# Block 2's stage meetings and mixers: low parts of the second unit last, another order of attention steps, lighter VectorE work, rotary row swaps by DMA

## The reference, cut to what matters

```python
def second_block(x, c, ...):
    for l in range(2):
        h = _rmsnorm(x, norm_g[l, 0]) * (1.0 + sc0) + sh0
        x = x + 0.5 * g0 * _swiglu(h, ...)
        h = _rmsnorm(x, norm_g[l, 1]) * (1.0 + sc1) + sh1
        x = x + g1 * _token_mix(h, ...)
        h = _rmsnorm(x, norm_g[l, 2]) * (1.0 + sc2) + sh2
        x = x + 0.5 * g2 * _swiglu(h, ...)

def _rope(x, pos):                       # d = 32 or 64, half = d // 2
    x1, x2 = xf[..., :half], xf[..., half:]
    return jnp.concatenate([x1 * cos - x2 * sin, x2 * cos + x1 * sin], axis=-1)

def _diff_attention(q, k, v, lam, ...):  # 4 heads, two maps of 32 rows each
    s = jnp.einsum('bhmqd,bhmkd->bhmqk', qi, k) * scale
    p = _masked_softmax(s, causal)
    a = p[:, :, 0] - lam * p[:, :, 1]
    return a @ v

def _compress(x, pe, w1, w2):
    return jax.nn.silu(flat @ w1) @ w2

def _nsa(q, kc, vc, ks, vs, kw, vw, gates, pe, w1, w2):
    q = _rope(q); k_slc = _rope(ks); k_win = _rope(kw)
    k_cmp, v_cmp = _rope(_compress(kc)), _compress(vc)
    # compressed branch: masked softmax over 31 blocks (a row that sees none gives 0)
    # two more branches: causal softmax with k_slc and with k_win
    return g0 * o_cmp + g1 * o_slc + g2 * o_win
```

## Time and profile before

| | before |
|---|---|
| median of 3 runs | 2774.49 us |
| the profiled execution | 2776.58 us |
| its span | 2775.2 us |
| PE busy | 2712.5 us (98%) |
| DVE busy | 1667.2 us (60%) |
| ACT busy | 1024.0 us (37%) |
| mean granted TensorE clock | 0.992 |

### The profile page before, as it was taken

One profiled execution on the slowest core, in us unless ns is written; L12 is line 12 of the kernel. 1 busy time (PEld: TensorE's weight loads), 2 busy tenths in 40 slices (PEclk: granted clock), 3 DMA queues, 4 the chain that ended last, 5 costly groups with the idle time before them and its releaser, 6 DMA issues.

```text
span 2775.2 us, 35300 instructions
## 1 busy us (share of the span) xinstructions
PE 2712.5 (98%) x14529; PEld 2218.1 (80%) x14529; DVE 1667.2 (60%) x3377; ACT 1024.0 (37%) x1745; POOL 15.8 (1%) x47
## 2 busy tenths in 40 slices
PE   8999999999999999889999999999999989999999
PEld 5788888899888897666888889888888666888888
DVE  6776555357766456778776736753355778633334
ACT  4642332444222244455422224322234455422223
POOL 1000000000000000000000000000000000000000
PEclk9999999999999999999999999999999999999999
DMA  7246333224555232200555524533232310233231
GB/s 249 91 167 184 107 92 98 76 92 167 187 188 186 84 118 80 84 32 31 182 182 183 196 84 139 202 122 106 91 104 89 94 43 31 68 96 102 92 102 65
DMA packets 340360, 325.24 MB, mean 117 GB/s; under 512 B 9442, under 2 KB 332774, under 8 KB 340200
## 3 DMA queue, kind: packets, MB, share of 16 engines
q1 hardware_dynamic: 340116, 322.97, 36.1%
q10 hardware_dynamic: 84, 0.02, 0.0%
HBM read 320.87 MB, written 2.10 MB: 116 GB/s over the span
## 4 chain that ended last, share of the span: by engine, by line
PE 88%; DVE 7%; ACT 3%; SPq 1%; issue 0%; DMA 0%; DVEq 0%
PE bank L535 25%; PE bank L537 24%; PE bank L536 24%; PE bank L577 3%; PE bank L563 2%; PE bank L564 2%; PE bank L565 2%; PE bank L2319 1%; PE bank L2348 1%; DVE w_lo L503 1%; ACT E L2122 1%; PE bank L1373 1%; PE bank L1363 1%; DVE tmp L713 1%; DVE h_lo L702 1%; DVE E L2445 0%
## 5 line engine op out<-in xcount | busy, mean ns | idle before, releaser
L535 PE MATMUL bank<-h_lo,w_hi 128*128 128x512 f32 (+1 forms) x2448 | 929.4, 380 | 7.7 <-DVE h_lo L702 7.3
L537 PE MATMUL bank<-h_hi,w_lo 128*128 128x512 f32 (+1 forms) x2448 | 902.1, 369 | 0.0
L536 PE MATMUL bank<-h_hi,w_hi 128*128 128x512 f32 (+1 forms) x2448 | 901.1, 368 | 0.0
L503 DVE TENSOR_TENSOR w_lo<-raw,w_hi 128x1024 fp32r<-128x1024 f32 (+1 forms) x422 | 490.8, 1199 | 300.9 <-ACT w_hi L497 300.7
L497 ACT ACTIVATE w_hi<-raw 128x1024 fp32r<-128x1024 f32 (+1 forms) x422 | 421.5, 1035 | 341.9 <-PE bank L537 326.6
L535 PEld LDWEIGHTS bank<-h_lo,w_hi 128*128 128x128 f32 x2448 | 463.0, 189 | 94.7 <-issue 10.3
L536 PEld LDWEIGHTS bank<-h_hi,w_hi 128*128 128x128 f32 x2448 | 463.0, 189 | 79.3 <-issue 7.2
L537 PEld LDWEIGHTS bank<-h_hi,w_lo 128*128 128x128 f32 x2448 | 462.1, 189 | 77.5
L535 PE MATMUL bank<-a_lo,w_hi 128*128 128x512 f32 (+1 forms) x1056 | 390.8, 370 | 0.0
L537 PE MATMUL bank<-a_hi,w_lo 128*128 128x512 f32 (+1 forms) x1056 | 384.6, 364 | 0.0
L536 PE MATMUL bank<-a_hi,w_hi 128*128 128x512 f32 (+1 forms) x1056 | 384.4, 364 | 0.0
(11 more groups left out here) (311 smaller groups left out, 2600.1 us busy)
## 6 DMA issues: line engine op xcount, KB each, us to landing
swf<-in_w_ada SPq DMA_DIRECT2D x60, 1024.0 KB, 7.5
raw<-in_ffn_w_gate SPq DMA_DIRECT2D x44, 1024.0 KB, 5.4
raw<-in_ffn_w_up SPq DMA_DIRECT2D x44, 1024.0 KB, 5.4
raw<-in_w_in SPq DMA_DIRECT2D x40, 1024.0 KB, 5.1
raw<-in_ffn_w_down SPq DMA_DIRECT2D x32, 1024.0 KB, 5.0
raw<-in_w_in SPq DMA_DIRECT2D x34, 512.0 KB, 5.0
raw<-in_ffn_w_down SPq DMA_DIRECT2D x16, 768.0 KB, 4.2
mw<-in_w_mod SPq DMA_DIRECT2D x8, 1024.0 KB, 11.3
```

The source lines that it names most:

```text
L503: nc.vector.tensor_tensor(o, r, half(w_his[place_of[i]], i, h)[0].bitcast(F32), ALU.subtract).then_inc(*w_lo.up((i, h)))
L535: nc.tensor.matmul(o, w1, al, start=start, stop=False)
L536: nc.tensor.matmul(o, w1, ah, start=False, stop=False)
L537: return nc.tensor.matmul(o, w2, ah, start=False, stop=stop)
```

## The change

1. **Meetings.** `dve_w` of the second unit leaves slot 6 of `dve_modulate` and stands behind its last chunk.
2. **Rotary part of nq, ks and kw (six of ten units in each mixer).** The matmul is gone. SP copies the rows with four DMAs inside SBUF, 32 rows of 512 columns each, to `swap`, and the sign is in the sin table. DVE multiplies `swap` by sin and adds. For ks and kw one 128x512 sum goes out, and SP copies the second head group to the other half of the partitions with two DMAs each (`sp_cross`).
3. **Differential attention.** DVE makes the factors of step s-1 between map 0 and map 1 of step s; ACT scales map 0 of step s-1 between the two exponentials of step s, ahead of its copy.
4. **Silu of the hidden layer.** ACT makes it as Exp, Ln(1+z), Exp; two DVE instructions fall away. The second one comes a step earlier on ACT.
5. **Compressed branch.** `VB` is one 128x512 product with a quadrant mask in place of eight copies and POOL's clearing; the 0/1 mask over 256 columns becomes a factor of the 8 sums.

```diff
@@ dve_second, dve_to_h
-                3: [lambda: update(6)], 4: [lambda: dve_nacc(st, 6, 1)], 5: [lambda: update(7)],
-                6: [lambda: st != "end" and dve_w(first_of(st)[1], 0)]}
+                3: [lambda: update(6)], 4: [lambda: dve_nacc(st, 6, 1)], 5: [lambda: update(7)],}
...
             dve_modulate(st, 0, mu, add, dve_second(st, b4, gain))
+            dve_w(first_of(st)[1], 0)
@@ rope
+    def sp_rope(l, p):
+        sp.wait_ge(act, ("rq", l, p))
+        for i in range(4):
+            nc.sync.dma_start(swaps[p % 2][i * 32:i * 32 + 32, :], pair(p)[0][(i ^ 1) * 32:(i ^ 1) * 32 + 32, :]).then_inc(
+                *swap_in[p % 2].up((l, p), 16))
...
+        else:
+            q0 = swaps[p % 2]
+            dve.wait_ge(swap_in[p % 2], (l, p))
+            nc.vector.tensor_tensor(q0[:, :], q0[:, :], sin, ALU.mult).then_inc(*dve.up(("rs", l, p)))
@@ dve_da, act_da
+                    if m:
+                        factors(s - 1)
...
-                dve.wait_ge(act, ("de", l, n, 1))
-                nc.vector.reciprocal(st[:, 2:4], st[:, 2:4]).then_inc(*dve.up(("dr", l, n)))
-                dve.wait_ge(dve, PREV)
-                nc.vector.tensor_tensor(st[:, 3:4], st[:, 3:4], lv[:, 6:7], ALU.mult).then_inc(*dve.up(("dl", l, n)))
-                dve.wait_ge(dve, PREV)
+                dve.wait_ge(dve, ("dl", l, n))
...
+                    if m:
+                        first_map(s - 1)
@@ silu
+        act.wait_ge(act, PREV)
+        nc.scalar.activation(z, z, use(ACT.Ln), bias=ones[0:64, 0:1]).then_inc(*act.up(("h4", l, m)))
+        act.wait_ge(act, PREV)
+        nc.scalar.activation(z, z, use(ACT.Exp), scale=-1.0).then_inc(*act.up(("hs", l, m)))
...
-        nc.vector.tensor_scalar(z, z, 1.0, None, ALU.add).then_inc(*dve.up(("h3", l, m)))
-        nc.vector.reciprocal(z, z).then_inc(*dve.up(("h4", l, m)))
@@ dve_vc, dve_nsa
-                nc.vector.tensor_copy(VB[g][r, q * 64:q * 64 + 64], ps.of(("hv", l))[r, g * 64:g * 64 + 64]).then_inc(
+        nc.vector.tensor_tensor(VB[:, :].rearrange("p (g q d) -> p g q d", g=2, q=4),
...
-                nc.vector.tensor_tensor(e3, e3, c01, ALU.mult).then_inc(*dve.up(("cz", l, b)))
@@ pe_mixer
-        pe_rope(l, 4)
         compressing(0, 0)
-        pe_rope(l, 5)
@@ sp_mixer
+        swap_after = {("nq", l, 0): (4, 5), ("nq", l, 1): (6, 7), ("kk", l): (8, 9)}
         for n in names[index["dk", l]:index["vv", l]]:
             sp_raw(index[n] + 2)
+            for p in swap_after.get(n, ()):
+                sp_rope(l, p)
+            if n == ("ng", l):
+                sp_cross(l)
+    def sp_cross(l):
+        for n, kd in enumerate((ks, kw)):
+            sp.wait_ge(dve, ("rd", l, 8 + n))
+            for par in range(2):
+                r, o = slice(par * 64, par * 64 + 64), slice(64 - par * 64, 128 - par * 64)
+                nc.sync.dma_start(kd[r, 512:1024], kd[o, 0:512]).then_inc(*cross_in[n].up(l, 16))
```

More of the change, by code:

```diff
@@ L52, in host_constants @@
     c["ca"] = m(ok).transpose(1, 0, 2).reshape(128, 128)
-    c["c01"] = ok.astype(np.float32).transpose(1, 0, 2).reshape(128, 128)
+    c["any"] = ok.any(2).astype(np.float32).T
+    c["quad"] = (p[:, None] // 32 == np.arange(4)[None, :]).astype(np.float32)
     res = np.concatenate([c[n] for n in RES], 1)
@@ L69, in table @@
         return np.ascontiguousarray(co.T[rows]), np.ascontiguousarray(si.T[rows])
-    l2 = np.concatenate([*table(64, np.arange(S)), *table(64, end)], 1)
+    co, si = table(64, np.arange(S))
+    si = np.where((p % 64 < 32)[:, None], -si, si)
+    l2 = np.concatenate([co, si, *table(64, end)], 1)
     return {"k_res": res.astype(np.float32), "k_l1": l1.astype(np.float32), "k_l2": l2.astype(np.float32),
             "k_da": np.concatenate(table(32, np.arange(S)), 1)}
-RES = ["ident", "ones", "bones", "tril", "C", "R32", "R64", "ca", "c01"]
-RESW = {"C": 512}
+RES = ["ident", "ones", "bones", "tril", "C", "R32", "R64", "ca", "any", "quad"]
+RESW = {"C": 512, "any": 4, "quad": 4}
 PREV = "prev"
@@ L373, in build @@
     kcz = here("kcz", 128)
-    VB = [here(f"VB{i}", 256) for i in range(2)]
+    VB = here("VB", 512)
     hid, hsum = [here(f"hid{i}", 128) for i in range(2)], here("hsum", 256)
@@ L389, in build @@
     dk = sb("dk", 1024, at=at_a + 8192)
+    swaps = [sb(f"swap{i}", 512, at=at_a + 16384 * i + 12288) for i in range(2)]
     groups = vector_rows(A)
@@ L1957, in build @@
     ld_ws, ld_bs = sig("ws_in"), sig("bs_in")
+    swap_in = [sig(f"swap{i}_in") for i in range(2)]
+    cross_in = [sig(f"cross{i}_in") for i in range(2)]
     PAIR = {("dq", 0): 0, ("dq", 1): 1, ("dk", 0): 2, ("dk", 1): 3, ("n0", 0): 4, ("n0", 1): 5, ("n1", 0): 6,
@@ L1978, in rope_where @@
         else:
-            kd = (ks, kw)[p - 8]
-            d = [(slice(g * 64, g * 64 + 64), kd[par * 64:par * 64 + 64, g * 512:g * 512 + 512])
-                 for g in range(2) for par in range(2)]
+            d = [(every, (ks, kw)[p - 8][:, 0:512])]
         return t, d
@@ L1992, in pe_rope @@
         pe.wait_ge(act, ("rq", l, p))
-        nc.tensor.matmul(t[:, :], rope_where(l, p)[0][0], pair(p)[0][:, :], start=True, stop=True).then_inc(
+        nc.tensor.matmul(t[:, :], cst["R32"], pair(p)[0][:, :], start=True, stop=True).then_inc(
             *pe.up(("rr", l, p)))
     def dve_rope(l, p):
-        (_, cos, sin), dsts = rope_where(l, p)
+        (cos, sin), dsts = rope_where(l, p)
         q0, q1 = pair(p)
@@ L2079, in dve_da, with factors @@
     def dve_da(l):
+        def factors(n):
+            if n < 0:
+                return
+            st = sts[n]
+            dve.wait_ge(act, ("de", l, n, 1))
+            nc.vector.reciprocal(st[:, 2:4], st[:, 2:4]).then_inc(*dve.up(("dr", l, n)))
+            dve.wait_ge(dve, PREV)
+            nc.vector.tensor_tensor(st[:, 3:4], st[:, 3:4], lv[:, 6:7], ALU.mult).then_inc(*dve.up(("dl", l, n)))
         for s in range(22):
@@ L2114, in act_da, with first_map @@
     def act_da(l):
+        def first_map(n):
+            if n < 0:
+                return
+            E0 = E5[2 * n % 7][:, 0:(DA_ITEMS[n][1] + 1) * 128]
+            act.wait_ge(dve, ("dr", l, n))
+            nc.scalar.activation(E0, E0, ACT.Copy, scale=sts[n][:, 2:3]).then_inc(*act.up(("dk", l, n)))
         for s in range(22):
@@ L2123, in act_da @@
                                          accum_out=st[:, 2 + m:3 + m]).then_inc(*act.up(("de", l, s, m)))
+            if s == 16:
+                first_map(15)
             da_copy(act, l, s - 3)
[L2125 to L2130, removed]
             if s in (11, 19):
@@ L2553, in act_nsa @@
             nsa_copy(act, l, s - 3)
-            if s == 1:
+            if s == 0:
                 act_hidden_silu(l, 1)
@@ L2899, in pool_mixer @@
             pool.wait_ge(dve, ("acc", ada_end[b4]))
-        for i, t in enumerate((kcz, *VB)):
-            nc.gpsimd.memset(t[:, :], 0.0).then_inc(*pool.up(("zn", l) if i == 2 else ("zn", l, i)))
+        nc.gpsimd.memset(kcz[:, :], 0.0).then_inc(*pool.up(("zn", l)))
         pool.wait_ge(ld_ws, l)
```

47 lines of the change are left out of this document (23 added, 24 removed).

## The result

The changed kernel takes a median of 2738.39 us (2737.67 to 2739.44 over 4 runs); the kernel before, run beside it, 2774.39 us. The ratio is 0.987, with a 95% interval of 0.9853 to 0.9887: 36.0 us less, 1.3%. The forecast was 2730 us, 44.5 less, with a range of 2717 to 2752. The time lies inside the range and 8 us above the forecast.

The account below looks back on a forecast made before the run. The prediction took PE, busy for 98% of the span, as the bound, its waits ended mostly by VectorE. Terms of 10.4, 4.0, 18.0, 8.8 and 3.7 sum to 44.9 us off 2776.58, giving 2730 us, range 2717 to 2752.

Parts of the forecast that it names:

- Term 1: In the two mixers, twelve rotary matmuls of 0.87 us each leave PE: 10.4 us gained.
- Term 2: At stage meetings, low parts put last bring the h_lo chunks sooner, with new w_lo waits of 0.55 us: 4.0 us gained.
- Term 3: In differential attention, VectorE's chain shortens 15.2 us per mixer, removing PE's idle time (12.4) and low clock (5.6): 18.0 us gained.
- rival A: In differential attention VectorE's waits for ACT do not shorten, so only 25.0 us are gained, 2749.5 us; chance 0.17.
- Term 4: In sparse attention, lighter silu, mask and VB work shortens PE's waits by 4.4 us per mixer: 8.8 us gained.
- Term 5: In sparse attention, shorter waits give back 40% of the 9.1 us cost of low clock: 3.7 us gained.
- The swaps: Row-swap DMAs before VectorE's sin product, landing in 3 to 4 us under at least 7.1 us of cover: no cost.
- Rival B: PE's waits and low clock all but vanish: 56.2 us gained, 2718 us; chance 0.12.

Follow-up runs that it names:

- the light part alone: The kernel before, with only the silu's reciprocal and addition on ACT, VB in one instruction and the mask product as a factor: 2766.29 us, ratio 0.9965.
- the small fill: The changed kernel with one unread 128x512 product ahead of the scores of step 3 of sparse attention: 2737.4 us, ratio 0.9863 to the kernel before.
- the copy first: The changed kernel with VectorE's copy put ahead of the two minima at steps 3 and 9 of sparse attention: 2735.91 us, ratio 0.9853.

## Why the prediction was right, and where it was off

Against the profiled execution of before, 2776.58 us, the terms stand so: forecast 44.9, measured 37.1.

- **Term 1** (10.4): held. The accounts of the stages in the changed kernel, with swaps alone and with swaps undone close to within about 1.5 us with 5.2 us for each mixer.
- **Term 2** (4.0): 4.1 in the changed kernel, 4.3 alone. The new waits for `w_lo` are 0.52 and 0.51 us; 0.55 was worked out.
- **Term 3** (18.0): 9.5 us of idle time and 6.3 of clock, 15.8. The clock was put at 5.6, the idle time at 12.4. The sum was near for a reason that was only half right. It set VectorE's shortening (15.2 us for each mixer) against PE's shortfall (15.5), as if all of it counted. The steps alone gave VectorE 20.8 us in both mixers and the kernel 6.1, with no low clock gone. What brought more than forecast were the swaps: with the rotary product went the waits for its bank and the low clock behind them. And 4.2 us of the idle time that stayed are waits for ACT's copies, 0.99 and 1.11 us in each mixer:

```profile
1109.09 0.44 PE L582 MATMUL bank<-res,E 128*128 128x128 f32 x2 [0.99 <-ACT tmp L2091]
...
1135.48 0.55 PE L582 MATMUL bank<-res,E 128*128 128x128 f32 x3 [1.11 <-ACT tmp L2091]
```

  The sum had left 0.9 us for each mixer, and had made VectorE the only laggard; that ACT's copies come behind the scaling was said under rival A, but priced in no term. The kernel before has 3.2 us of such waits, one of 2.21 us and one of about 1, which the reading that VectorE ends nearly all of them passed over; the new order alone leaves one of 2.19 us, and the light part alone two of 2.24.
- **Term 4** (8.8): 7.8. The two long waits were forecast at 1.9 and 2.6 us and are 2.09 and 2.76; the one for `gmb` went from 4.6 to 0.2 in all.
- **Term 5** (3.7): 1.4 between the two profiled executions, and this is the step whose reason failed. In sparse attention PE was busy for 15.8 us at half clock, 18.7 before (the prediction read 18.2); half of the difference is what PE's busy time fell by. The reason given (the waits that stay lie between 1.2 us, behind which the clock stayed, and 3.0, behind which it fell, so 40% comes back) took the length of the wait as what decides. The waits of 2.09 and 2.76 us stand in six kernels here (the changed one, the light part alone, steps undone, swaps undone, the small fill, the swaps four times), so in twelve mixers. Behind the first the clock stayed high once (with the small fill, where the wait of 0.88 us ahead of it was filled), was low for 3.4 us six times and for 6.8 us five times; behind the second, longer one it stayed high four times and was low for 3.4 us eight times. And behind 1.67 us, in the kernel with the copy first, it was low for 6.8 us in both mixers. So the length of a wait does not tell what follows it.

  The size varies as much: the six kernels were at half clock for 13.7 us on the average (10.2 to 17.1), and the four with sparse attention as it was before (the kernel before, the meetings, the swaps and the steps alone) for 23.0 us (20.5 to 27.3), of which PE was busy for 13.3 and 20.2. On these averages the clock gave back 3.4 us, near the 3.7 forecast, but that is luck, since the interpolation behind it does not hold. The Trainium skill (TensorE: Matmul & The Clock Gate, A second HAM failure mode: psum-queue depth-cycling), by which this term would be 0, speaks of frequent short idle times between groups of matmuls; here the short ones alone did nothing, as the kernels with filled waits show: in the mixers, low clock began only where a wait of 1.59 us or more had just ended or was under way.
- **The swaps** cost nothing, as forecast. They land in 2.0 us (the bounds were 2.1 and 5.4), as the DMA rows of the changed kernel show, in KB each and us to landing:

```profile
swap<-tmp SPq DMA_DIRECT2D x48, 64.0 KB, 2.0
```

  The Trainium skill's fit (DMA: Bandwidth & Descriptors, Anatomy of one DMA — SWDGE (gpsimd) path) is for DMAs issued by GpSimd, while these are SyncE's; worked out for 64 KB it gives 2.15 us, an estimate, and the 2.0 us here agree with it. But SP takes 0.6 us to issue one, so some 2.4 for four, where the prediction had 1.8. From ACT's copy to the last landing a unit takes 3.8 to 5.1 us, the same 3.9 as a round of the kernel with four of them. Unit 5 has 8.0 us of cover and used 4.8 and 3.8 of them.

So 7.8 us were missing: 2.2 of term 3, 1.0 of term 4, 2.3 of term 5, and 1.5 lost at block 1's start, outside the change. The 0.9 that is left, with 0.1 that term 2 gave beyond its forecast, is in no term: between and behind the mixers the kernel became 3.0 us shorter where PE's idle time fell by 3.6, and 0.3 more came ahead of the first mixer. Rival A (2749.5) is refuted by its own row: VectorE's waits for the scaling in both mixers went from 35.9 to 15.5 us. Rival B was not reached even later: with the waits filled and the copy first, at 2731.6 us, no low clock is left in the mixers, and that is still 13.6 above its 2718, since idle time stays.

What stays open: why a wait of the same length, at the same place, was followed by low clock in one mixer and not in the other; whether several short waits add up; and whether the parts help each other, since 31.7 and 36.0 us can't be told apart. The light part was not undone on the changed kernel.

## What to carry to other kernels

Shortening the engine that seems the laggard pays only at the places where the bound engine waits for it. Of 20.8 us taken off VectorE's waits, 6 reached the end. Twelve products of 0.87 us that had to wait for their bank to be freed, taken from the bound engine, shortened the stage by 14.0 us, more than their 10.4 (VectorE's lighter sums came with them). Where PE's waits of 1.6 us or more can't be removed, work that nobody reads, put in their place, was worth 7 us here.

## What the runs showed of the hardware

- In sparse attention no stretch of low clock (1.2 GHz instead of 2.4) began behind a wait of up to 1.54 us, nor behind pairs of 0.87 and 0.80 or 1.53 and 0.99 us a few us apart. Behind 1.67 us (with 0.88 us of idle time 3 us before) the clock was low for 6.8 us in both mixers, and behind 2.1 us from nothing to 6.8. In differential attention with the swaps alone, the clock was high behind waits of 2.48 and 2.46 us, and with the old order of steps 3.4 us of low clock began 1.5 us behind one of 1.59 us, in one mixer of two. The length of a wait alone doesn't tell.
- Behind a single wait low clock lasted 3.4 or 6.8 us, a cost of 1.7 or 3.4 us, and the longer wait (2.76 us) had the shorter stretches.
- PE rows that count as busy can hide a wait for the second bank of a pair: 3.6 us for a group that took 2.8 before.
- A swap of four DMAs of 64 KB within SBUF took 3.8 to 5.1 us from ACT's copy to the last landing, though one DMA lands in 2.0 us: 0.6 us went by for each issue. Four such rounds on one queue, each behind the landing of the one before, took 16 us or more, and the next unit's rounds began behind them.
